# Two attentions' inverse row sums: one wide reciprocal and one transpose in place of two spreading products

## The reference, cut to what matters

```
s = scores(q, k) + bias            # 128 queries x up to 1024 keys
p = exp(s - rowmax(s))
o = (p @ v) / rowsum(p)            # the division is what the change touches
mixed = concat(o_a * silu(z_a), o_b * silu(z_b))
```

## Time and profile before

| | |
|---|---|
| median of 3 runs | 2491.68 us (2490.99 to 2492.49) |
| span of the profiled execution, first to last instruction | 2489.4 us |
| PE busy | 2407.7 us (97%) |
| DVE busy | 1100.2 us (44%) |
| ACT busy | 712.3 us (29%) |
| mean granted TensorE clock | 0.990 |
| first attention | about 2042 to 2177 us |
| second attention | about 2230 to 2387 us |

### The profile page before, as it was taken

The page is one execution under the profiler, slowest core; times in us unless marked ns, Lnnn a source line. Parts: engine busy times, 40 slices in busy tenths (PEclk is TensorE's granted clock), DMA queues, the critical chain, the costliest instruction groups (busy, mean ns, idle before and its releaser), DMA issues.

```text
span 2489.4 us, 36188 instructions
## 1 busy us (share of the span) xinstructions
PE 2407.7 (97%) x15614; PEld 1906.9 (77%) x15614; DVE 1100.2 (44%) x1352; ACT 712.3 (29%) x1096; POOL 1016.8 (41%) x677
## 2 busy tenths in 40 slices
PE   7999999999999989999999999999999999989999
PEld 6888777777779868878888887888677876656677
DVE  5140113223186355676676664334333216655521
ACT  4101122232222122254344431012322015564411
POOL 4323323323223368577777763444622310002221
PEclk9999999999999999999999999999999999999999
DMA  5111322222210146423222225221113121000014
GB/s 195 50 44 44 97 80 77 85 68 81 67 31 4 46 145 210 136 68 93 85 76 82 88 97 182 102 86 59 49 36 110 43 68 39 1 24 12 1 60 127
DMA packets 208248, 189.82 MB, mean 76 GB/s; under 512 B 16714, under 2 KB 186929, under 8 KB 207834
## 3 DMA queue, kind: packets, MB, share of 16 engines
q1 hardware_dynamic: 208090, 187.51, 24.2%
HBM read 141.31 MB, written 45.13 MB: 75 GB/s over the span
## 4 chain that ended last, share of the span: by engine, by line
PE 89%; DVE 6%; ACT 2%; POOL 1%; issue 1%; DMA 0%; SPq 0%; DVEq 0%; POOLq 0%; ACTq 0%
PE gp L1113 14%; PE gp L1115 13%; PE gp L1114 13%; PE sm L1598 3%; PE sm L1599 3%; PE sm L1600 3%; PE gp L1598 3%; PE gp L1599 3%; PE gp L1600 3%; PE gp L1693 2%; PE gp L1709 2%; PE sm L1809 2%; PE gp L1627 2%; PE sm L1628 2%; PE sm L1627 2%; PE sm L1629 2%
## 5 line engine op out<-in xcount | busy, mean ns | idle before, releaser
L1113 PE MATMUL gp<-h_hi,w_hi 128*128 128x512 f32 x1264 | 508.4, 402 | 1.3 <-ACT k_sb L1921 1.3
L878 POOL CAST w_hi<-w_raw 128x1024 fp32r<-128x1024 f32 (+1 forms) x121 | 130.8, 1081 | 918.3 <-PE gp L1115 537.6
L1115 PE MATMUL gp<-h_hi,w_lo 128*128 128x512 f32 x1264 | 493.8, 391 | 0.0
L1114 PE MATMUL gp<-h_lo,w_hi 128*128 128x512 f32 x1264 | 493.5, 390 | 0.0
L880 POOL TENSOR_TENSOR w_lo<-w_raw,w_hi 128x1024 fp32r<-128x1024 f32 (+1 forms) x129 | 341.9, 2650 | 10.3 <-ACT w_hi L2049 0.5
L1113 PEld LDWEIGHTS gp<-h_hi,w_hi 128*128 128x128 f32 x1264 | 237.8, 188 | 70.8 <-issue 23.7
L1114 PEld LDWEIGHTS gp<-h_lo,w_hi 128*128 128x128 f32 x1264 | 238.0, 188 | 51.2 <-issue 4.3
L1115 PEld LDWEIGHTS gp<-h_hi,w_lo 128*128 128x128 f32 x1264 | 237.8, 188 | 50.9
L2445 DVE TENSOR_TENSOR_SCAN sb_run<-sb_keep,ones_row 128x128 f32<-128x128 f32 (+7 forms) x32 | 77.1, 2449 | 318.1 <-POOL sb_keep L925 318.1
L1046 POOL TENSOR_TENSOR w_lo<-w_sum,w_hi 128x512 fp32r<-128x512 f32 x66 | 96.4, 1461 | 45.8 <-ACT w_hi L2108 45.8
L2269 ACT ACTIVATE att_s<-att_s,small 128x1024 f32<-128x1024 f32 (+7 forms) x128 | 98.7, 773 | 10.6 <-DVE small L2918 10.2
(11 more groups left out here) (528 smaller groups left out, 5232.3 us busy)
## 6 DMA issues: line engine op xcount, KB each, us to landing
w_raw<-in_w_in SPq DMA_DIRECT2D x79, 512.0 KB, 4.4
gates_spill<-gate_out SPq DMA_DIRECT2D x32, 512.0 KB, 3.1
gate_in<-gates_spill SPq DMA_DIRECT2D x30, 512.0 KB, 4.3
w_raw<-in_w_up SPq DMA_DIRECT2D x22, 512.0 KB, 5.0
up_raw<-in_w_up SPq DMA_DIRECT2D x22, 512.0 KB, 5.0
g_spill<-hid SPq DMA_DIRECT2D x22, 512.0 KB, 2.6
g_stage<-g_spill SPq DMA_DIRECT2D x22, 512.0 KB, 4.4
w_raw<-in_w_down SPq DMA_DIRECT2D x22, 512.0 KB, 3.6
```

What stands on the lines that cost most here:

```text
L878: pool.tensor_copy(w_hi[:, t % 2, 0:n], w_raw[:, t % 2, 0:n]).then_inc(s["w_high"], 1)
L1113: pe.matmul(o, wh, hi[:, k0 + k, c], start=(k == 0), stop=False)
L1114: pe.matmul(o, wh, lo[:, low[k] if low else k0 + k, c], start=False, stop=False)
L1115: mm = pe.matmul(o, wl, hi[:, k0 + k, c], start=False, stop=(k == n - 1))
```

## The change

VectorE no longer writes the reciprocals as two columns. It reads each of the two sums 64 times over (a stride of zero) and writes the reciprocals over 128 columns of a new tile `share_t`, four of which take turns. TensorE turns that tile with one transpose, which gives the same content in `at_share_place()` as the two products gave. The transpose stands at the end of `turn(u)`, and so ahead of `z(u+3)`; the two products stood in `output(u)`, behind it. The waits for `at_root` and for `at_o_taken` of unit `u-1` are there now too; `output(u)` keeps its own wait for `at_o_taken`. `share_t` lies on the memory of `lora`, which the first layer uses.

```diff
+        share_t = at("share_t", [P, 4, P], F32, base[0])
         lora = fixed("lora", [P, 2, BW])
...
                 def turn(u):
...
                         mm.then_inc(s["at_pt"], 1)
+                    pe.wait_ge(s["at_root"], u + 1)
+                    if u >= 1:
+                        pe.wait_ge(s["at_o_taken"], u)
+                    pe.transpose(at_share_place(), share_t[:, u % 4, :], ident[:, :])
 
                 def output(u):
                     if u >= 1:
                         pe.wait_ge(s["at_o_taken"], u)
                     j, qb = at_unit(u)
-                    pe.wait_ge(s["at_root"], u + 1)
-                    for hh in range(2):
-                        pe.matmul(at_share_place()[C * hh:C * hh + C, :], at_small(2, u, hh).to_broadcast([P, C]),
-                                  ident[:, :], start=True, stop=True, skip_group_check=True)
...
                 def roots(u):
                     dve.wait_ge(s["at_p"], 2 * (u + 1))
-                    dve.reciprocal(at_small(2, u), at_small(1, u)).then_inc(s["at_root"], 1)
+                    if u >= 4:
+                        dve.wait_ge(s["at_o"], u - 3)
+                    dve.reciprocal(share_t[:, u % 4, :].rearrange("p (h c) -> p h c", h=2),
+                                   at_small(1, u).unsqueeze(2).to_broadcast([P, 2, C])).then_inc(s["at_root"], 1)
```

## The result

The changed kernel takes 2542.23 us (median of 4, 2540.45 to 2544.07), the kernel before beside it on the same chip 2491.34 us. The ratio is 1.0204, with a 95% interval of 1.019 to 1.0218: 50.9 us slower. The profiled execution has a span of 2540.9 us, 51.5 more. The forecast was 2541 us.

The account below looks back on a forecast made before the run. The loop of scores between TensorE and VectorE was taken to set the attentions' pace. Longer pairs +48.8, last units -3.4, starts +2.4, ends +1.2 gave +49 on 2491.7: 2541 us, range 2509 to 2558.

Parts of the forecast that it names:

- The price of the reciprocal: VectorE's 128-column reciprocal between its two passes over the scores: 0.97 us, 0.81 more than the narrow one.
- rival A: Cheap wide reciprocal on VectorE, only 0.13 us more than the narrow one: +21 us, 2513 us; chance 0.15.
- The moved wait: TensorE's next scores wait for VectorE's gate products and the transpose: 1.05 us, where today it is 0.14.
- The two paths: In each unit, scores to next scores takes the longer of VectorE's and TensorE's path: +5.91 or +6.30 us a pair.
- k' = 8: Unit 6, with scores of width 8: scores to next scores 6.24 us in the first attention, 7.32 in the second.
- rival B: TensorE idles more in the attentions and its clock falls to 1.2 GHz: 14 us more, 2555 us; chance 0.05.
- The sign that was set for it: In the profile's attentions, a granted clock below 0.9 would show the slower TensorE clock.
- the standstill in unit 6: TensorE stands for some 2 us within the 6.24 us step of the unit with scores of width 8.
- The terms for starts and ends: At the attentions' edges: last three units -3.4 us, starts +2.4, ends +1.2.
- The net of removed and added work on TensorE: Two products removed (0.2 us), one transpose added (0.107): 0.1 us less a unit, 6 to 7 us in all.

Follow-up runs that it names:

- p_widths: The kernel before with reciprocals of 2 to 512 columns, two products by a constant and a spreading copy behind VectorE's last work; only its profile used, 128 columns 953 ns.
- e2: The kernel before with its two spreading products and their waits moved ahead of the scores, reciprocal still 2 columns: 2514.88 us, +24.7.
- e3: The changed kernel with a 2-column reciprocal that ScalarE copies over 128 columns, transpose still ahead of the scores: 2507.69 us, +17.5.
- e4: The changed kernel with eight unused identity products in TensorE's longest wait, in the unit with 16 turns: 2534.01 us, +43.7.
- e1: The changed kernel with its transpose put back behind the scores, wide reciprocal still between the two passes: 2512.41 us, +22.2.
- e7: The kernel before with its narrow reciprocal spread by ScalarE and one transpose replacing the two products, behind the scores: 2494.82 us, +4.5.
- e8: The changed kernel with the wide reciprocal done twice, the second waiting for the first: 2604.53 us, +114.3.
- e5: The kernel before with its 2-column reciprocal moved from between the two passes to behind the gate products: 2487.43 us, -2.9.
- e9: The changed kernel with only the wide reciprocal moved, from between the two passes to behind the gate products: 2523.93 us, +33.7.

## Why the prediction was right

**The price of the reciprocal.** Forecast 0.97 us, measured 0.947. That is 0.79 more than the narrow one takes, where 0.81 was taken; the two passes together with it grew by 0.74 (2.36 to 3.10). The slope of the same operation between its own widths was the right row to go by; the ordinary product of that width (287 ns) would have led to rival A. A second record of 8 columns in p_widths (204) shows that the single one was sound. But the two narrow records by themselves give 7.0 ns a column and 1.04 us, against the 6.25 of p_widths, and 0.97 was a choice between this and a lower figure that had another reason. That it lies within 0.02 us is in part luck.

**The moved wait.** Forecast 1.05 us from the gate products to the next scores, measured 0.98. That the wait alone costs as much as it does is shown by e2 and e3 (+24.7 and +17.5; rival A, made real by e3, was put at +21).

**The two paths.** The steps forecast for the first attention against those of the timeline: 6.24 and 6.10 for k' = 8; for the whole pair 37.56 and 36.82. In the second attention 7.32 and 7.19, and 43.36 for the pair against 42.70, in pairs without the slower clock. So the paths were 0.7 us a pair too long in both attentions, 5.6 us over the eight pairs: the pairs were to cost 48.8 us, and at full clock they cost 4 x (36.82 - 31.65) + 4 x (42.70 - 37.06) = 43.2. Where VectorE sets the pace the step is some 0.13 too long (6.24 against 6.10), of which 0.07 lies behind the gate products and 0.07 in the two passes.

**The clock.** The forecast left it out of the sum, and kept it as rival B at 0.05, with a price of 14 us. It is there, in five of the eight pairs, at 1.52 us each in the first attention and 1.56 in the second: 2 x 1.52 + 3 x 1.56 = 7.7 us. The sign that was set for it, a granted clock below 0.9 in the attentions, did not show it: the means are 0.95 (2040 to 2185) and 0.97 (2290 to 2450), and only the short stretches fall to 0.5. I had taken the standstill in unit 6 as the one that counts. In the changed kernel the products that slowed stand behind the longer wait for VectorE's copy in the next unit with 16 turns, 2.5 us; only in e4, with that one filled, does the clock fall behind unit 6, in three pairs.

The forecast's 49 us against 50.9 is thus closer than its parts, and that is luck: 5.6 us too many in the paths, and 7.7 missing for the clock. The two together leave 2.1, and the measured time lies 1.9 above the sum. The terms for starts and ends, +0.2 in all, were not taken apart by any run.

**The pieces do not add up, and should not.** Place alone +17.5 (e3), wide reciprocal alone +22.2 (e1), together +50.9, which is 11 more than the sum. Neither piece is quite alone: e3 has ScalarE's copies and e1 the transpose behind the scores, which without held scores and wide reciprocal are +4.5 together (e7). Counted from e7, the place adds 13.0, the reciprocal 17.7, and both 46.4. The two paths give a reason: with the scores not held, TensorE's path is the longer one in units 1, 3, 5 and 7, and hides part of the reciprocal; with the scores held, VectorE's path is the longer one nearly everywhere, and takes the reciprocal in full (the step of e8 above, +0.98). The slower clock comes on top, and in e3 it was not seen between the first products and the last. The pairs of the first attention at full clock bear the paths out: 31.65 before, 33.45 in e3, 33.77 in e1, 36.82 in the changed kernel, so both together cost 1.25 us a pair more than the sum, 5 of the 11 us over four pairs. In the second attention e1 has no whole pair at full clock, and the other 6 us were not split.

**The net of removed and added work on TensorE** was taken as 0.1 us less a unit. For the place that the change chose it fits: the step from the scores with k' = 3, which TensorE paces, was forecast at 3.93 us with it and takes 3.91 (2139.25 to 2143.16). In the other place e7's steps are 0.03 to 0.05 us longer, not 0.1 shorter. Only the steps that TensorE paces hold this term.

## What to carry to other kernels

Before work is moved ahead of something in an engine's queue, list the waits that move with it: here 0.1 us of TensorE's time brought a wait for two gate products to the front of the scores, and +17 us came of it alone (e3). Spread after the expensive operation, not before it: 128 columns of reciprocals took 947 ns, and two columns with a copy that spreads them 388. And when an instruction must be put somewhere in a tight queue, what stands between two halves of the work that the other engine waits for is the dearest place (e5, e9).

## What the runs showed of the hardware

VectorE's reciprocal in 32-bit floats takes 6.25 ns a column and some 150 ns beside that, from 2 to 512 columns; a product by a constant takes 226 ns for 128 columns. Useless products can pay: with eight of them in a wait of some 2.5 us, the kernel was 7.2 us faster by its medians and 5 by its trace, since TensorE's granted clock stayed up behind that wait; in three of eight pairs it then fell behind a standstill of some 1.84 us, behind which the changed kernel had kept its full clock. A single 128x128 transpose between products of another cut takes 0.26 us of TensorE from its load to the next one, more than the two half-width products of four records that it replaced (0.16); the steps grew by 0.03 to 0.05.
